# Four page products moved to a head's end, and the norm of the out-projection with narrow sums, in place

## What is computed

```python
hn = rmsnorm(x, lp['norm_mix'])
q, k, v, f_logit, xr, gr = jnp.split(hn @ lp['w_in'], SPLIT_IDX, axis=-1)
logf = jax.nn.log_sigmoid(f_logit + lp['b_forget'])
att = attention(q, k, v, logf).reshape(b, t, D_ATT)      # 8 heads of 64
rnn, h_last, rnn_conv_new = rg_lru_branch(xr, gr, rnn_conv_buf, rnn_h0, lp)
merged = jnp.concatenate([rmsnorm(att, lp['norm_att_out']), rmsnorm(rnn, lp['norm_rnn_out'])], axis=-1)
x = x + merged @ lp['w_out']
f, ffn_new = gated_conv_ffn(rmsnorm(x, lp['norm_ffn']), ffn_buf, lp)
x = x + f
```

## Time and profile before

| | us |
|---|---|
| runs | 3356.98, 3363.46, 3363.10 |
| median | 3363.1 |
| profiled execution | 3355.78 |
| its span, first to last instruction | 3353.6 |

### The profile page before, as it was taken

How to read it: one execution, slowest core, us unless ns; L and a number is a source line. 1 busy time by engine, 2 the same in 40 slices (tenths; PEclk the granted TensorE clock), 3 DMA queues, 4 the chain that set the end, 5 groups by cost and what they waited for, 6 DMA issues and landing times.

```text
span 3353.6 us, 46822 instructions
## 1 busy us (share of the span) xinstructions
PE 3037.8 (91%) x15400; PEld 2659.0 (79%) x15400; DVE 1447.2 (43%) x1910; ACT 757.9 (23%) x1529; POOL 1212.9 (36%) x575
## 2 busy tenths in 40 slices
PE   4798998957788888897899999999999998999998
PEld 4798987843354545455898999999999998999998
DVE  4212433348566555534415445555445554222221
ACT  5100332212232333333202000000000002434343
POOL 1011111133566565633766222222222222455443
PEclk7899999967799898998899999999999999999999
DMA  5211343355787677754345111111111114555553
GB/s 182 94 65 55 90 104 94 86 106 160 237 250 231 182 228 236 229 174 136 113 132 154 44 47 51 51 42 48 45 42 51 51 38 155 183 182 188 180 194 110
DMA packets 253580, 422.52 MB, mean 126 GB/s; under 512 B 49265, under 2 KB 156954, under 8 KB 248906
## 3 DMA queue, kind: packets, MB, share of 16 engines
q1 hardware_dynamic: 167986, 322.58, 30.8%
q10 hardware_dynamic: 85152, 97.07, 9.6%
q0 software_dynamic: 288, 1.05, 0.1%
HBM read 337.21 MB, written 83.46 MB: 125 GB/s over the span
## 4 chain that ended last, share of the span: by engine, by line
PE 69%; DMA 7%; POOL 7%; DVE 6%; issue 5%; SPq 4%; ACT 2%; ACTq 0%; POOLq 0%; DVEq 0%
PE PS L2452 33%; PE PS L2154 13%; PE PS L2534 4%; PE PS L2536 4%; PE PS L2535 4%; POOL prod L905 3%; DMA Kpg<-in_cache_k 2%; PE PS L2346 2%; SPq L581 2%; PE PS L2443 1%; SPq L574 1%; DMA xin<-in_x_prompt 1%; PE PS L2135 1%; DVE YT L2097 1%; DMA mixT<-RX 1%
## 5 line engine op out<-in xcount | busy, mean ns | idle before, releaser
L2452 PE MATMUL PS<-MH,VS 128*128 128x416 f32 x4000 | 1086.9, 352 | 11.2 <-POOL VS L968 9.0
L2452 PEld LDWEIGHTS PS<-MH,VS 128*128 128x128 f32 x4000 | 750.1, 188 | 23.2 <-issue 12.3
L2452 PE MATMUL PS<-ML,VS 128*128 128x416 f32 x2000 | 701.4, 351 | 0.0
L962 POOL TENSOR_TENSOR VR<-VR,gains 128x1024 f32<-128x1024 f32 x52 | 98.7, 1898 | 791.6 <-PE PS L2452 694.9
L2452 PEld LDWEIGHTS PS<-ML,VS 128*128 128x128 f32 x2000 | 376.7, 188 | 4.2 <-issue 0.8
L1025 POOL TENSOR_TENSOR DL<-DR,DH 128x1408 fp32r<-128x1408 f32 x80 | 258.6, 3233 | 286.1 <-ACT DH L1446 286.0
L905 POOL TENSOR_TENSOR prod<-Kpg,qb 128x1024 f32<-128x1024 f32 x118 | 284.0, 2407 | 174.0 <-DMA Kpg<-in_cache_k 137.9
L2346 PE MATMUL PS<-PT,VA 128*65 128x416 f32 (+16 forms) x816 | 340.0, 501 | 4.0 <-ACT PT L1307 3.5
L2534 PE MATMUL PS<-GH,DH 128*128 128x416 f32 x880 | 314.3, 357 | 16.2 <-DVE GL L2079 8.6
L2154 PE MATMUL PS<-XH,WH 128*128 128x416 f32 x840 | 307.2, 366 | 19.8 <-issue 11.6
L2536 PE MATMUL PS<-GH,DL 128*128 128x416 f32 x880 | 310.5, 353 | 0.0
(11 more groups left out here) (273 smaller groups left out, 4501.7 us busy)
## 6 DMA issues: line engine op xcount, KB each, us to landing
Kpg<-in_cache_k SPq DMA_DIRECT2D x256, 256.0 KB, 4.2
Vpg<-in_cache_v SPq DMA_DIRECT2D x256, 256.0 KB, 4.1
DR<-in_w_down SPq DMA_DIRECT2D x80, 704.0 KB, 4.1
gT<-GO ACTq DMA_DIRECT2D x110, 208.0 KB, 1.9
VR<-in_w_up SPq DMA_DIRECT2D x44, 512.0 KB, 3.5
GRb<-gT SPq DMA_DIRECT2D x31, 416.0 KB, 5.1
WR<-in_w_stream SPq DMA_DIRECT2D x21, 512.0 KB, 3.6
GRa<-gT SPq DMA_DIRECT2D x24, 416.0 KB, 5.8
```

Of the source, the lines that this page charges most:

```text
L2452: mm = e.matmul(PS[:, j, 0:BW], w[:, u, k], x[:, k, cols(j)], start=(k == 0 and q == 0), stop=(k == KC - 1 and q == 2))
```

## The change

- **Heads 1 to 6.** POOL makes the first four products for sample i + 2 at the end of head i, behind the last one for sample i + 1; in the head itself it makes six, then prepares, then six more (before: eight and eight). DVE's reductions sit at `SCORES_AT`, the last at tile 33 (before 38), and the sample's *end* at tile 36 (before 40). `load_order` moves key groups 8 to 23 to suit, asks for the next head's values at 14 (20) and the query at 17 (31), and for its rows at 30.2 (23).
- **Norm.** Loads go into `MF` itself, with a semaphore for each block; no load waits for a buffer, and blocks 3 and 4 are loaded before the residuals. The sum is 16 products of 104 columns (`QW`) in four groups of 32 rows of one bank: each group holds one half of the columns of one of the two sums. Root and reciprocal then work on 104 columns in place of 416. A new step `norm_spread` brings them back to 128 rows with four products by the selection matrix `pick`, and `norm_apply` reads its factor from PSUM. DVE takes over four of the eight chunks of `norm_low`. A Sqrt of one column stands ahead of the first square.
- **Order.** ACT squares one block ahead, not two. On PE each first dense block is followed by one sum and one spread. Residual additions and squares come two blocks later.
- **Weights.** `split_v` is cut into `gain_v` and `halve_v`. For chunk 2 the gain comes ahead of squares 3 and 4, the halves behind them; everywhere the gain no longer waits for the halves' buffer.

```diff
@@ -128,6 +126,9 @@
 ENDS = [max(t for t, tile in enumerate(TILES) if tile[0] == j) for j in range(NB)]
+SCORES_AT = (2, 3, 5, 6, 8, 10, 11, 12, 14, 15, 25, 27, 28, 30, 31, 33)
@@ -170,14 +171,14 @@
         if not last:
-            plan[8 + 3 * g // 2 if g < 8 else 28 + 3 * (g - 8) // 2].append(("scores", 16 + g))
+            plan[SCORES_AT[g]].append(("scores", 16 + g))
 if first:
...
                     (50, "sums")) if first else \
-            ((40, "end"), (42, "turn"), (43, "top"), (44, "spread max"), (45, "less"), (46, "exps"), (48, "sums")):
+            ((36, "end"), (42, "turn"), (43, "top"), (44, "spread max"), (45, "less"), (46, "exps"), (48, "sums")):
         plan[t].append((step, 1))
@@ -190,13 +191,14 @@
     found += [(at + 0.5, "v", 2 * b + 4), (at + 0.5, "v", 2 * b + 5)]
-for n in range(4, 20):
+for n in range(4 if first else 8, 24):
     if first:
...
     else:
-        at = 5.2 + 1.5 * (n - 4) if n < 12 else 26 + 1.5 * (n - 12)
+        at = 5.2 + 1.5 * (n - 8) if n < 14 else 21.5 + 1.5 * (n - 14) if n < 20 else 37 + 1.5 * (n - 20)
     found.append((at, "k", n))
-found += [(20, "values", 0), (23, "head", 0), (31, "query", 0)]
+found += [(20, "values", 0), (23, "head", 0), (31, "query", 0)] if first else \
+    [(14, "values", 0), (17, "query", 0), (30.2, "head", 0)]
 return [step[1:] for step in sorted(found)]
@@ -596,7 +604,7 @@
 for what, n in order:
-    if what == "k" and n < 8 + 8 * min(more, 1) + 4 * (more > 1) and more:
+    if what == "k" and n < 8 + 8 * min(more, 1) + 8 * (more > 1) and more:
         fetch_keys(i + 1 + n // 16, n % 16)
@@ -705,12 +708,14 @@
 fetch_v(1, 1)
+for n in range(3, 5):
+    fetch_norm(n)
 for k in range(NB):
     fetch_first_residual(k)
-for n in range(3, 10):
+for n in range(5, 10):
     fetch_norm(n)
-    if n >= 8:
-        fetch_first_residual(n - 3)
+for k in range(5, 7):
+    fetch_first_residual(k)
 e.wait_ge(v_lo, 1)
@@ -935,43 +940,63 @@
 pool_products(1, 1, 0, 16)
-with e.Fori(0, 3) as ii:
+pool_products(2, 0, 0, 4)
+def pool_head(i, v, more=True):
+    e.wait_ge(pv, 51 * i + 1)
+    e.wait_ge(kpp, 16 * i + 20 - DVE_FIRST)
+    prepare(i + 1, v, 0, 3)
+    e.wait_ge(prep, 7 * i + 10)
+    pool_products(i + 1, v, 4, 10)
+    e.wait_ge(kpp, 16 * i + 26 - DVE_FIRST)
+    prepare(i + 1, v, 3, 7)
+    e.wait_ge(prep, 7 * i + 14)
+    pool_products(i + 1, v, 10, 16)
+    if more:
+        pool_products(i + 2, 1 - v, 0, 4)
+with e.Fori(0, 2) as ii:
     for v in range(2):
-        i = 2 * ii + 1 + v
-        e.wait_ge(pv, 51 * i + 1)
-        prepare(i + 1, v, 0, 3)
-        e.wait_ge(prep, 7 * i + 10)
-        pool_products(i + 1, v, 0, 8)
-        prepare(i + 1, v, 3, 7)
-        e.wait_ge(prep, 7 * i + 14)
-        pool_products(i + 1, v, 8, 16)
+        pool_head(2 * ii + 1 + v, v)
+pool_head(5, 0)
+pool_head(6, 1, False)
 e.wait_ge(kpp, 16 * NS - DVE_FIRST)
...
-def split_v(m, u, of_out=False):
+def gain_v(m, u):
...
     e.wait_ge(v_ld[u], 16 * (m // 2) + 16 if isinstance(m, int) else 8 * (m - u) + 16)
+    if not (isinstance(m, int) and m < 2):
+        e.wait_ge(v_lo, m - 1)
+    e.sem_inc(go, 1)
+    gain = gains[:, 0:KC] if isinstance(m, int) and m < 8 else gains[:, KC:2 * KC]
+    e.tensor_tensor(VR[:, u], VR[:, u], gain.unsqueeze(2).to_broadcast([P, KC, P]), ALU.mult)                    .then_inc(v_gn, 1)
+def halve_v(m, u):
     if isinstance(m, int) and m == 2:
...
         e.wait_ge(u_mm, 5 * m - 5)
-    e.sem_inc(go, 1)
-    gain = gains[:, 0:KC] if of_out or isinstance(m, int) and m < 8 else gains[:, KC:2 * KC]
-    e.tensor_tensor(VR[:, u], VR[:, u], gain.unsqueeze(2).to_broadcast([P, KC, P]), ALU.mult)\
-        .then_inc(v_gn, 1)
     e.wait_ge(v_gn, m + 1)
...
+def split_v(m, u):
+    gain_v(m, u)
+    halve_v(m, u)
 def norm_low(n):
...
     e.wait_ge(nhi, n + 1)
-    e.tensor_tensor(ML[:, :, c], MF[:, :, c], MH[:, :, c].bitcast(F32), ALU.subtract)\
+    e.tensor_tensor(ML[:, 0:4, c], MF[:, 0:4, c], MH[:, 0:4, c].bitcast(F32), ALU.subtract)\
         .then_inc(nlo, 1)
@@ -991,15 +1016,22 @@
+pool.inc(e.memset(pick[:], 0.0))
+pool.settle()
+pool.inc(e.affine_select(out=pick[:], in_=pick[:], compare_op=ALU.not_equal, fill=1.0, base=0,
+                         pattern=[[-32, 4], [0, P]], channel_multiplier=1))
 split_v(0, 0)
...
     norm_low(n)
-    if n >= 5:
-        square(n - 5, (n - 5) // 2, (n - 5) % NB, (n - 5) % 2 == 0)
+    if n >= 7:
+        square(n - 7, (n - 7) // 2, (n - 7) % NB, (n - 7) % 2 == 0)
+gain_v(2, 0)
+for k in range(3, 5):
+    square(k, k // 2, k % NB, k % 2 == 0)
+halve_v(2, 0)
 for k in range(5, 10):
     square(k, k // 2, k % NB, k % 2 == 0)
-split_v(2, 0)
 split_v(3, 1)
@@ -1340,18 +1372,16 @@
-s = n % NRS
-e.wait_ge(nr_ld[s], norm_landed(n))
+e.wait_ge(mix_ld[n], mix_at[n])
 if n == 9:
     e.wait_ge(na_s, 1)
-e.activation(SQ[:, :, cols(n, HB)], NR[:, s], ACT.Square).then_inc(nsq, 1)
+e.activation(SQ[:, :, cols(n, HB)], MF[:, :, cols(n, HB)], ACT.Square).then_inc(nsq, 1)
...
 if n >= 2:
-    e.wait_ge(nst, n - 1)
-e.activation(NG[:, n % 2], PS[:, 5 + n % 2, 0:2 * HB].rearrange("p (a n) -> p a n", a=2),
-             ACT.Sqrt, bias=epsT[:], scale=2 / DM).then_inc(nrs, 1)
+    e.wait_ge(nsp, nsp0 + n - 1)
+e.activation(NG[:, n % 2], PS[:, 5, 0:QW], ACT.Sqrt, bias=epsT[:], scale=2 / DM).then_inc(nrs, 1)
@@ -1380,18 +1410,18 @@
+e.activation(warm[:], epsT[:], ACT.Sqrt)
 norm_square(0)
-norm_square(1)
 for n in range(10):
     norm_root(n)
+    if n < 9:
+        norm_square(n + 1)
     if n:
         norm_high(n - 1)
-    if n < 8:
-        norm_square(n + 2)
-    if n >= 4:
-        store_first_sum(n - 4)
+    if n >= 7:
+        store_first_sum(n - 7)
 norm_high(9)
-for k in range(6, 10):
+for k in range(3, 10):
     store_first_sum(k)
@@ -1938,15 +1968,24 @@
-def norm_apply(n):
+def norm_invert(n):
...
     e.reciprocal(NG[:, n % 2], NG[:, n % 2]).then_inc(nrc, 1)
-    e.wait_ge(nrc, n + 1)
-    e.tensor_tensor(
-        MF[:, :, cols(n, HB)].rearrange("p (a k) n -> p a k n", a=2),
-        NR[:, n % NRS].rearrange("p (a k) n -> p a k n", a=2),
-        NG[:, n % 2].unsqueeze(2).to_broadcast([P, 2, KC // 2, HB]), ALU.mult).then_inc(nst, 1)
+def norm_apply(n):
+    e.wait_ge(nsp, nsp0 + n + 1)
+    x = MF[:, :, cols(n, HB)].rearrange("p (a k) n -> p a k n", a=2)
+    gain = PS[:, 6 + n % 2, 0:2 * HB].rearrange("p (a n) -> p a n", a=2)
+    e.tensor_tensor(x, x, gain.unsqueeze(2).to_broadcast([P, 2, KC // 2, HB]), ALU.mult).then_inc(nst, 1)
+def norm_low(n):
+    c = cols(n, HB)
+    e.wait_ge(nhi, n + 1)
+    e.tensor_tensor(ML[:, 4:8, c], MF[:, 4:8, c], MH[:, 4:8, c].bitcast(F32), ALU.subtract)\
+        .then_inc(nlo_dve, 1)
@@ -1971,17 +2010,16 @@
+e.tensor_copy(MF[:, 0:4, TPR:TP], attS[:]).then_inc(na_s, 1)
 for n in range(10):
+    norm_invert(n)
+    if n:
+        norm_low(n - 1)
     norm_apply(n)
-    if n == 5:
-        e.wait_ge(nst, 6)
-        e.wait_ge(nr_ld[9 % NRS], norm_landed(6))
-    if n == 6:
-        e.wait_ge(nst, 7)
-        e.tensor_copy(NR[:, 9 % NRS, 0:4, TPR - 9 * HB:HB], attS[:]).then_inc(na_s, 1)
-    if n >= 3:
-        add_first_residual(n - 3)
-for k in range(7, 10):
+    if n >= 5:
+        add_first_residual(n - 5)
+norm_low(9)
+for k in range(5, 10):
     add_first_residual(k)
@@ -2420,18 +2458,28 @@
     e.wait_ge(nsq, n + 1)
+    if n:
+        e.wait_ge(nrs, n)
+    for q in range(KC // 2):
+        for g in range(4):
+            o = n * HB + (g % 2) * QW
+            mm = e.matmul(PS[32 * g:32 * g + 32, 5, 0:QW], onesF[:, 0:32],
+                          SQ[:, KC // 2 * (g // 2) + q, o:o + QW], start=(q == 0), stop=(q == KC // 2 - 1))
+    mm.then_inc(nmm, 1)
+def norm_spread(n):
+    e.wait_ge(nrc, n + 1)
     if n >= 2:
-        e.wait_ge(nrs, n - 1)
-    for k in range(KC):
-        p, q = divmod(k, KC // 2)
-        mm = e.matmul(PS[:, 5 + n % 2, p * HB:(p + 1) * HB], onesF[:], SQ[:, k, cols(n, HB)],
-                      start=(q == 0), stop=(q == KC // 2 - 1))
-    mm.then_inc(nmm, 1)
+        e.wait_ge(nst, n - 1)
+    for g in range(4):
+        mm = e.matmul(PS[:, 6 + n % 2, QW * g:QW * g + QW], pick[:, g], NG[:, n % 2], start=True, stop=True)
+    mm.then_inc(nsp, 1)
...
     e.wait_ge(x2_acc, NT + 35 + j + 1)
-    e.wait_ge(nrs, 10 + j - 1)
+    e.wait_ge(nrs, max(10 + j - 1, 10))
     e.matmul(PS[:, 5 + j % 2, 0:BW], onesF[:], R2[:, cols(j)], start=True, stop=True).then_inc(nmm, 1)
@@ -2454,15 +2502,21 @@
+norm_total(0)
+e.wait_ge(c_pool, 16)
 for n in range(3):
-    norm_total(n)
+    norm_total(n + 1)
+    norm_spread(n)
+e.wait_ge(v_lo, 2)
 for j in range(NB):
-    for n in range(2 * j + 3, min(2 * j + 5, 10)):
-        norm_total(n)
-    e.wait_ge(v_lo, 2)
     e.wait_ge(nlo, 2 * j + 2)
-    first_dense(2 * j)
-    first_dense(2 * j + 1)
+    e.wait_ge(nlo_dve, nlo0 + 2 * j + 2)
+    for k in (2 * j, 2 * j + 1):
+        first_dense(k)
+        if k + 4 < 10:
+            norm_total(k + 4)
+        if k + 3 < 10:
+            norm_spread(k + 3)
```

(2 more changed lines are left out.)

36 lines of the change are left out of this document (18 added, 18 removed).

## The result

| | before | after |
|---|---|---|
| median of 4 runs, us | 3363.28 | 3323.61 |
| lowest to highest | 3356.98 to 3367.15 | 3320.62 to 3332.74 |
| profiled execution | 3355.78 | 3320.62 |
| its span | 3353.6 | 3318.9 |

The changed kernel takes 0.9881 of the time before, with an interval of 0.9855 to 0.9907: 40 us faster. The forecast was 3263, 100 us faster, and its range ended at 3302. The direction was right and the norm's part came out as forecast. The heads gave 14.8 us by the two traces for the 70 that were forecast.

A forecast was written before the change was run, and what follows sets the result against it. It took POOL's late page products, which hold up DVE and PE in the heads, and the norm's chain behind them as bounds. Profiled 3355.8 - 70 (heads) - 26 (norm) = 3259.8, with half of 7.3 added: 3263 us; range 3240 to 3302.

The forecast's parts named there:

- the 70 that were forecast: Heads 1 to 6: us saved by moving four of POOL's 16 products to the end of the head before.
- Norm, 26 us: Norm and start of chunk 2: shorter sums and block chains, no gap or slow start, save 26 us (bounds 18 and 32).
- POOL's last product at 52.1: In a head, POOL's last own product ends 52.1 us after the start, against 73.5 before.
- tiles 30 to 36 in 9 to 10 us: Sign in each head: PE goes from tile 30 to 36 in 9 to 10 us, for 14.9 before.
- which then land about 66 us into the head, while PE wants them at tile 42, at 65.7: 0 to 2 us lost: Heads: value groups 12 and 13, loaded behind the next head's rows, cost PE 0 to 2 us.
- Rival 1: Heads: SP's in-order queue holds back key or value pages; heads of 87 us, 65 saved in all, 3294; chance 0.18.
- For this and the value pages I add 2 us: Heads: allowance for tight DVE at tiles 2 to 16 and late value pages, raising 79.3 to 81.5 us a head.
- saved 561.1 - 491.5: Heads: present stretch of 561.1 us less forecast 84 + 5 x 81.5 = 491.5, giving 70 us.
- my 81.5: Forecast time in us of each head but the first of the six, which was given 84.
- six tiles at 47.3/30: Heads, tiles 30 to 36: priced at the pace of the 47.3 us up to tile 30, written as 9.7 us.
- Clock near 1.00: Sign: the granted clock of the heads rises from 0.91 to near 1.00.
- The floor of 79.3: Heads: PE's fastest segments put end to end, 79.3 us a head; as a bound it saves 85 us.

The follow-up runs named there:

- e1: The changed kernel with all edits of the heads undone, so the norm's part alone: 3340.35 us, 0.9937 of the kernel before.
- e3: The changed kernel with the next head's rows loaded behind value groups 12 and 13: 3307.41 us, 0.9843 of the kernel before.
- e6: e3 with DVE's multiplication of the last head's output moved from tile 16 to 22, its store to 24: 3297.33 us, ratio 0.9800.
- e10: e9 with POOL's first product for a sample waiting for DVE's maximum of the sample before, two counts later: 3282.26 us, ratio 0.9764.
- e9: e6 with the next head's rows loaded behind value groups 14 and 15 too: 3296.06 us, 0.9803 of the kernel before.
- e11: e10 with the loop over heads 1 to 6 written out on PE, DVE and ACT: 3273.99 us, ratio 0.9734.
- e12: e11 with loads of the next head's values and the query behind value groups 8 and 9: 3272.67 us, ratio 0.9720.

## Why the prediction was wrong, step by step

- **Norm, 26 us: right.** 25 by the trace (22.8 + 2.4), 21 [14, 29] by e1. Sum 0.92 for 1.0, spread 1.14 for 0.9, multiply 1.89 for 2.0, blocks of 6.5 to 6.8 us for 6.4, first dense block and chunk 2 at 19.0 and 83.7 for 19 and 83. The Trainium skill, TensorEngine Tiling (Array Packing), "Key Properties", says that a change of tiling mode drains TensorE. These rows don't show a drain by itself: the sum at 1565.73 has no idle time before it, and a block, with a change into the narrow groups and one out of them, takes 0.1 to 0.4 us more than the 6.4 forecast, which the spread's 1.14 for 0.9 alone could make up.
- **POOL's last product at 52.1, tiles 30 to 36 in 9 to 10 us: right** (54.9; 8.5 to 9.0).
- **"which then land about 66 us into the head, while PE wants them at tile 42, at 65.7: 0 to 2 us lost": the mis-sized term.** In head 4 they were there at 74.9. I gave the rows no time in the DMA queues and took the median of 4.2 us; behind the rows it was 11. Worth 18 us in the heads (e3), 13 to 16 in the time. Rival 1 had named the queue, at a chance of 0.18. Its heads of 87 would cost 33 us over the forecast, more than the rows did, so the queue alone doesn't give the measured time.
- **"For this and the value pages I add 2 us": the step that failed.** I counted DVE's work as fixed. It grew, in the stretch of the earlier trace rows, from 322.2 to 366.2 us, because the change put POOL's subtractions beside DVE's multiplication at tile 16, and its products beside the softmax steps. The change lost 14 us at tiles 13 to 19, where e6 against e3 then took away 28.6; tiles 36 to 42 gave 15.7 in e10 against e9, and PE waits 4.1 longer at head 0's end. These are sums of single intervals: of the 28.6, 18.8 were left in the heads, of the 15.7, 11.0.
- **"saved 561.1 - 491.5": two counting errors.** 561.1 is a stretch, and the six heads in it took 551.1: 10 us were put down as saved that aren't in the heads at all. And they hold two turns of the loop (crossings of 22.9 and 16.9 us for 13.0), while my 81.5 was built from head 4, which has none: another 13.8 us that the change doesn't touch. That left 46 of the 70. e11 shows that the crossings can be had at 13 us, though most of it came back elsewhere. A small slip beside them: six tiles at 47.3/30 are 9.5 us, not 9.7.
- **Clock near 1.00: wrong**, 0.91, with PE still waiting at tile 42. It rose as the waits went: from 938 to 1420 it was 0.91 in the changed kernel, 0.93 in e3, 0.95 in e6, 0.97 in e10 and 0.98 in e11 and e12.
- The floor of 79.3 could nearly be reached: 80.8, by four more edits (rows, multiplication, the wait for the maximum, the turns). It was no bound, though: with the multiplication moved, tiles 13 to 19 take 9.0 us for its 10.6. What the prediction lacked most were the waits behind the first one.

## What to carry to other kernels

When a change moves an engine's work in time, list what the other engine of a shared resource does at the new place: here POOL's subtractions of 4.6 us and products of 2.4 us met DVE operations that take 0.2 to 2.3 alone, and each paid the rest of the POOL instruction. A queue in order has to be walked with the bytes ahead of each load, not only with the waits: value pages behind 2.1 MB of rows were there after 11 us, where a load took 4. And a unit used to price all others (head 4) must hold what the others hold, loop turns included, and the stretch that it is taken from must begin and end with whole units.

## What the hardware showed that I had not expected

- DVE steps of 8 columns with two SBUF inputs take 1.6 to 2.4 us beside POOL's products for 0.17 alone; also a step with one SBUF input and a constant (L1792, 1.58 for 0.18) and the cast L1897 (2.01 for 1.47). Reductions (1.21 before and after) and operations with one input in PSUM (the multiply of 1664 columns at 1.89) don't pay.
- A crossing with a turn of the loop over two heads took 4 to 12 us longer than one without (16.9 to 24.7 for 13.0), in part as idle time without a releaser (PE 6.1, ACT 3.8). Written out, both crossings took 12.9; most of the gain came back at later tiles.
- 32 passes of 128 x 104 columns into four groups of 32 rows take 0.92 us at the high level of the clock (granted 1.00 around 1566 us) and 1.61 at the low one (0.50 from 1539 to 1552).
